# First layer's modulation in channel chunks, four column groups of TensorE, three projection units side by side

## The reference, cut to what matters

```python
cond_act = jax.nn.silu(cond)
shift, scale, gate = jnp.split(cond_act @ w_mod[layer] + b_mod[layer], 3, axis=-1)
hm = rmsnorm(x, norm_g[layer]) * (1 + scale[:, None]) + shift[:, None]
out = fc_mixer(hm, ...)      # layer 0: proj = h @ w_in, 1024 x 6144
x = x + gate[:, None] * out
```

## Time and profile before

| | |
|---|---|
| median of 3 runs | 1208.44 us (1207.91 to 1212.69) |
| profiled execution | 1208.46 us |
| its span | 1206.5 us |
| mean granted TensorE clock | 0.987 |
| TensorE busy | 94% |
| VectorE busy | 66% |
| ScalarE busy | 37% |
| GpSimd busy | 23% |
| HBM read | 134.31 MB |

### The profile page before, as it was taken

How to read it: one execution, slowest core, us unless ns; L and a number is a source line. 1 busy time by engine, 2 the same in 40 slices (tenths; PEclk the granted TensorE clock), 3 DMA queues, 4 the chain that set the end, 5 groups by cost and what they waited for, 6 DMA issues and landing times. The chain is left out here.

```text
span 1206.5 us, 19283 instructions
## 1 busy us (share of the span) xinstructions
PE 1134.3 (94%) x7179; PEld 1042.9 (86%) x7179; DVE 790.4 (66%) x1385; ACT 441.6 (37%) x846; POOL 279.9 (23%) x422
## 2 busy tenths in 40 slices
PE   6799999999999999999999999998999898978997
PEld 1389999999999998888899988998899898967885
DVE  1553444467666434547779796979797979776454
ACT  3331222121211123235534544453545354544321
POOL 1110000000000000013043533445353535454001
PEclk9899999999999999999999999999999999989999
DMA  8642223154544243314234333434342425272702
GB/s 332 190 145 69 85 87 104 54 180 123 169 127 152 88 162 105 95 35 157 72 101 131 101 112 106 127 102 126 93 122 85 131 76 156 68 268 65 298 26 87
DMA packets 175674, 148.11 MB, mean 123 GB/s; under 512 B 6844, under 2 KB 156708, under 8 KB 175220
## 3 DMA queue, kind: packets, MB, share of 16 engines
q1 hardware_dynamic: 170996, 130.29, 34.8%
q0 software_dynamic: 4608, 16.83, 4.2%
HBM read 134.31 MB, written 12.78 MB: 122 GB/s over the span
## 5 line engine op out<-in xcount | busy, mean ns | idle before, releaser
L261 DVE TENSOR_TENSOR w_lo<-raw_w,w_hi 128x1024 fp32r<-128x1024 f32 x128 | 157.0, 1230 | 94.4 <-ACT w_hi L255 92.8
L290 PE MATMUL PS<-h_hi,w_hi 128*128 128x320 f32 x768 | 177.0, 312 | 6.2 <-DVE h_lo L364 5.2
L290 PE MATMUL PS<-h_lo,w_hi 128*128 128x320 f32 x768 | 175.6, 310 | 0.0
L290 PE MATMUL PS<-h_hi,w_lo 128*128 128x320 f32 x768 | 175.4, 310 | 0.0
L255 ACT ACTIVATE w_hi<-raw_w 128x1024 fp32r<-128x1024 f32 x128 | 134.2, 1051 | 111.3 <-PE PS L290 72.2
L290 PEld LDWEIGHTS PS<-h_hi,w_hi 128*128 128x128 f32 x768 | 128.3, 188 | 11.3 <-issue 4.0
L1320 PE MATMUL PS<-h_hi,w_hi 128*128 128x320 f32 x480 | 118.9, 329 | 12.5 <-DVE big L1509 7.1
L290 PEld LDWEIGHTS PS<-h_hi,w_lo 128*128 128x128 f32 x768 | 129.0, 188 | 0.0
L290 PEld LDWEIGHTS PS<-h_lo,w_hi 128*128 128x128 f32 x768 | 128.9, 188 | 0.0
L1320 PE MATMUL PS<-h_hi,w_lo 128*128 128x320 f32 x480 | 111.4, 314 | 0.0
L1320 PE MATMUL PS<-h_lo,w_hi 128*128 128x320 f32 x480 | 111.1, 313 | 0.0
(11 more groups left out here) (223 smaller groups left out, 2250.2 us busy)
## 6 DMA issues: line engine op xcount, KB each, us to landing
raw_w<-in_fc_w_in_dram SPq DMA_DIRECT2D x48, 512.0 KB, 4.0
raw_w<-in_ssd_w_in_dram SPq DMA_DIRECT2D x48, 512.0 KB, 5.2
big<-l_scr SPq DMA_DIRECT2D x40, 512.0 KB, 4.3
big<-in_w_mod_dram POOLq DMA_DIRECT2D x16, 1024.0 KB, 5.4
raw_w<-in_fc_w_out_dram SPq DMA_DIRECT2D x16, 512.0 KB, 3.4
raw_w<-in_ssd_w_out_dram SPq DMA_DIRECT2D x16, 512.0 KB, 7.9
big<-in_w_mod_dram SPq DMA_DIRECT2D x6, 1024.0 KB, 18.0
y_scr<-big SPq DMA_DIRECT2D x40, 128.0 KB, 1.8
```

The source lines that it names most:

```text
L261: dve.tensor_tensor(w_lo[:, slot, :], raw_w[:, slot, :], w_hi[:, slot, :].bitcast(F32), ALU.subtract).then_inc(lo_ready, 1)
L290: mm = pe.matmul(PS[:, 2 * pair + s, 0:HALF], w[:, slot, ws], h[:, kt, s * HALF:(s + 1) * HALF], start=(kt == 0 and n == 0), stop=(kt == K ...
```

## The change

The eight pieces by k become four chunks by channels: chunk c holds shift and scale of channels 256c to 256c+255, for all eight k tiles (2 MB in two loads, rows of 1 KB). Two chunks fit in memory at once, so that chunks 2 and 3 wait until 0 and 1 are used.

- `mod_pe(c)`: eight matmuls, k tile t to column group t mod 4 (partitions 32q and up of PSUM bank 6), two k tiles added up in each group. The weights are the conditioning vectors padded with zeros to 32 columns (`condp`).
- `mod_copy_act(c)` copies the bank (128 by 512) to memory, and `mod_T_pe(c)` multiplies each 128 by 128 block of it by a new constant (`group_sum`), which adds the four groups and puts channels on partitions. `ss_dve(c)` makes scale and shift of two k tiles.
- Units 0, 1 and 2 run side by side in three pairs of PSUM banks, two k tiles at a time (`unit_part_pe`); chunk c+1's matmuls stand ahead of unit 0's part c, its sum between unit 0's and unit 1's. Unit 3 follows as before.
- The norm is done ahead of the modulation: SP loads x first, in five pieces, and ScalarE's queue the constants and conditioning vectors. Unit loads stand between chunks.
- On ScalarE `h_act` of the two k tiles of a chunk stands around the copy of the next chunk.

Other renamings and the waits that go with them are left out.

```diff
         xn = carve(5120 + 8192, 2, D)
         xT0 = carve(15360, KT, TOK)
-        mod_sb = carve(21504, 2 * D)
+        mod_sb = carve(25220, 2, 512)
         praw = carve(21504 + 2048, 2, P)
         praw3 = carve(23808, P)
...
-        def h_dve(dve, layer, xTb):
-            dve.wait_ge(xt_done, NT * (layer + 1) - 1)
-            dve.wait_ge(mod_ready, 2 * (layer + 1))
-            for k in range(KT):
-                for c, (a, b) in enumerate(SEGS):
-                    if k == 0 and c == 1:
-                        dve.wait_ge(xt_done, NT * (layer + 1))
-                    dve.tensor_scalar(xTb[:, k, a:b], xTb[:, k, a:b], ss_mod[:, 1, c, k:k + 1], ss_mod[:, 0, c, k:k + 1],
+        def ss_dve(dve, c):
+            ks = slice(2 * c, 2 * c + 2)
+            sel = PS[:, 7, 8 * c:8 * c + 8].rearrange("p (s k c) -> p s c k", s=2, c=2)
+            dve.wait_ge(mod_T, c + 1)
+            bias = par2[:, 56:72].rearrange("p (s k) -> p s k", s=2)[:, :, ks]
+            for s in range(2):
+                e = dve.tensor_tensor(ss_mod[:, s, :, ks], sel[:, s], bias[:, s].unsqueeze(1).to_broadcast([P, 2, 2]), ALU.add)
+            e.then_inc(ss_step, 1)
+            dve.wait_ge(ss_step, c + 1)
+            dve.scalar_tensor_tensor(out=ss_mod[:, 1, :, ks], in0=ss_mod[:, 1, :, ks], scalar=1.0,
+                                     in1=par2[:, ks].unsqueeze(1).to_broadcast([P, 2, 2]), op0=ALU.add, op1=ALU.mult).then_inc(ss_ready, 1)
+        def h_dve(dve, c):
+            dve.wait_ge(ss_ready, c + 1)
...
+                for seg, (a, b) in enumerate(SEGS):
+                    dve.tensor_scalar(xT0[:, k, a:b], xT0[:, k, a:b], ss_mod[:, 1, seg, k:k + 1], ss_mod[:, 0, seg, k:k + 1],
                                       ALU.mult, ALU.add).then_inc(v_done, 1)
-                if k % 2:
-                    dve.wait_ge(hh_done, KT * layer + k)
-                    dve.tensor_tensor(h_lo[:, k - 1, :], xTb[:, k - 1, :], h_hi[:, k - 1, :].bitcast(F32),
-                                      ALU.subtract).then_inc(h_ready, 1)
...
+            dve.wait_ge(hh_done, 2 * c + 1)
+            dve.tensor_tensor(h_lo[:, 2 * c, :], xT0[:, 2 * c, :], h_hi[:, 2 * c, :].bitcast(F32), ALU.subtract).then_inc(h_ready, 1)
...
+        def mod_pe(pe, c):
+            pe.wait_ge(wm_landed[c % 2], 32 * (c // 2) + 32)
+            if c:
+                pe.wait_ge(mod_copied, c)
+            for half in range(2):
+                for q in range(4):
+                    t = 4 * half + q
+                    mm = pe.matmul(PS[32 * q:32 * q + 32, 6, :].rearrange("p (s n) -> p s n", s=2), condp[:, t, :], wm[c % 2][:, :, t, :],
+                                   start=(half == 0), stop=(half == 1))
+            mm.then_inc(wm_used, 1)
+        def mod_T_pe(pe, c):
+            pe.wait_ge(mod_copied, c + 1)
+            if c:
+                pe.wait_ge(ss_step, c)
+            for j in range(4):
+                mm = pe.matmul(PS[:, 7, 8 * c + 2 * j:8 * c + 2 * j + 2], mod_sb[:, c % 2, j * P:(j + 1) * P], group_sum,
+                               start=True, stop=True)
+            mm.then_inc(mod_T, 1)
+        def mod_copy_act(act, c):
+            act.wait_ge(wm_used, c + 1)
+            if c >= 2:
+                act.wait_ge(mod_T, c - 1)
+            act.activation(mod_sb[:, c % 2, :], PS[:, 6, :], ACT.Copy).then_inc(mod_copied, 1)
+        def unit_part_pe(pe, u, c):
+            if c == 0:
+                pe.wait_ge(lo_ready, u + 1)
+            for kt in (2 * c, 2 * c + 1):
+                if u == 0:
+                    h_wait(pe, 0, kt)
+                ws = slice(kt * P, (kt + 1) * P)
+                for n, (w, h) in enumerate(((w_hi, h_hi), (w_hi, h_lo), (w_lo, h_hi))):
+                    for s in range(2):
+                        mm = pe.matmul(PS[:, 2 * u + s, 0:HALF], w[:, u, ws], h[:, kt, s * HALF:(s + 1) * HALF],
+                                       start=(kt == 0 and n == 0), stop=(kt == KT - 1 and n == 2))
...
         def start_pe(pe):
+            pe.wait_ge(cst_landed, 16)
+            for t in range(3):
+                norm_pe_tile(pe, t)
             pe.wait_ge(par_landed, 16 * PAR_DMAS)
             pe.transpose(PS[:, 6, 0:P], praw[:, 0, :], ident)
             pe.transpose(PS[:, 6, P:P + 72], praw[0:72, 1, :], ident[0:72, 0:72]).then_inc(par_T, 1)
-            pe.wait_ge(cond_ready, 1)
-            for s in range(8):
-                q, half = s // 2, s % 2
-                pe.wait_ge(wm_landed[s], 16)
-                for t in range(2):
-                    for b in range(2):
-                        mm = pe.matmul(PS[0:2, 2 * half + b, :], cond[:, :, 2 * q + t], wm[s][:, t, 512 * b:512 * b + 512],
-                                       start=(q == 0 and t == 0), stop=(q == 3 and t == 1))
-                mm.then_inc(wm_used, 1)
-                if 1 <= s < NT + 1:
-                    norm_pe_tile(pe, 0, xn, s - 1)
-        def start_pe_mod_T(pe):
-            pe.wait_ge(mod_copied, 2)
-            pe.wait_ge(xt_done, NT)
-            for j in range(16):
-                mm = pe.transpose(PS[:, 4, 2 * j:2 * j + 2], mod_sb[0:2, j * P:(j + 1) * P], ident[0:2, 0:2])
-            mm.then_inc(mod_T, 1)
+            for t in range(3, NT):
+                norm_pe_tile(pe, t)
+            pe.wait_ge(cond_padded, 1)
+            pe.wait_ge(par_ready, 2)
+            mod_pe(pe, 0)
+            mod_T_pe(pe, 0)
+            for c in range(4):
+                if c < 3:
+                    mod_pe(pe, c + 1)
+                unit_part_pe(pe, 0, c)
+                if c < 3:
+                    mod_T_pe(pe, c + 1)
+                unit_part_pe(pe, 1, c)
+                unit_part_pe(pe, 2, c)
         def fourier_pe(pe, i, first):
-            for k in range(4):
+            for k in range(3 if first else 0, 4):
                 pe.wait_ge(lo_ready, 4 * i + k + 1)
-                if not (first and k < 2):
-                    pe.wait_ge(act_freed, 4 * i + k - 1)
-                channel_tile(pe, k, k % 2, first and k == 0)
+                pe.wait_ge(act_freed, 4 * i + k - 1)
+                channel_tile(pe, k, k % 2)
...
-                src = pair_view(k % 2)
+                src = pair_view(2 if first and k == 2 else k % 2)
...
-            sp.dma_start(cond[:, 0, :], A["c"].rearrange("a (p t) -> (a p) t", t=KT)).then_inc(cond_landed, 16)
-            sp.dma_start(cond[:, 1, :], A["c_ctx"].rearrange("(p t) -> p t", t=KT)).then_inc(cond_landed, 16)
-            sp.dma_start(cst[:, :], A["consts"]).then_inc(par_landed, 16)
+            xs = A["x_sample"][0].rearrange("(t p) d -> p t d", p=P)
+            for t in range(NT):
+                sp.dma_start(x[:, t, :], xs[:, t, :] if t < 4 else A["x_prompt"][0]).then_inc(x_landed[t], 16)
             sp.dma_start(praw[0:96, 0, :], A["ssd_conv_w"].rearrange("a k (t n) -> (a k t) n", n=P)).then_inc(par_landed, 16)
             sp.dma_start(praw[96:128, 0, :], A["ssd_conv_b"].rearrange("a (t n) -> (a t) n", n=P)).then_inc(par_landed, 16)
             sp.dma_start(praw[0:16, 1, :], A["norm_g"].rearrange("a (t n) -> (a t) n", n=P)).then_inc(par_landed, 16)
             sp.dma_start(praw[16:40, 1, :], A["fc_conv_w"].rearrange("a k (t n) -> (a k t) n", n=P)).then_inc(par_landed, 16)
             sp.dma_start(praw[40:56, 1, :], A["ssd_norm_g"].rearrange("a (t n) -> (a t) n", n=P)).then_inc(par_landed, 16)
             sp.dma_start(praw[56:72, 1, :], A["b_mod"].rearrange("a (t n) -> (a t) n", n=P)[0:16, :]).then_inc(par_landed, 16)
-            xs = A["x_sample"][0].rearrange("(t p) d -> p t d", p=P)
-            for s in range(8):
-                if s == 7:
-                    sp.wait_ge(wm_used, 1)
-                q, half = s // 2, s % 2
-                sp.dma_start(wm[s], wm_src[0][:, 2 * q:2 * q + 2, 1024 * half:1024 * half + 1024]).then_inc(wm_landed[s], 16)
-                if s < 2:
-                    sp.dma_start(x[:, 2 * s:2 * s + 2, :], xs[:, 2 * s:2 * s + 2, :]).then_inc(x_landed[s], 16)
-                if s == 2:
-                    sp.dma_start(x[:, 4, :], A["x_prompt"][0]).then_inc(x_landed[2], 16)
-            for u in range(4):
-                if u % 2 == 0:
-                    sp.wait_ge(wm_used, 2 + u // 2)
+            def chunk_load(c):
+                if c >= 2:
+                    sp.wait_ge(wm_used, c - 1)
+                for s in range(2):
+                    sp.dma_start(wm[c % 2][:, s], wm_src[0][:, :, 1024 * s + 256 * c:1024 * s + 256 * c + 256]).then_inc(wm_landed[c % 2], 16)
+            def first_load(u):
                 sp.dma_start(raw_w[:, u, :], fc_src[:, :, fc_col(u):fc_col(u) + P]).then_inc(landed[u], 16)
-            sp.wait_ge(mod_ready, 2)
+            chunk_load(0)
+            first_load(0)
+            first_load(1)
+            chunk_load(1)
+            first_load(2)
+            chunk_load(2)
+            chunk_load(3)
+            first_load(3)
+            sp.wait_ge(wm_used, 4)
```

(82 more changed lines are left out.)

68 lines of the change are left out of this document (29 added, 39 removed).

## The result

| | before | after |
|---|---|---|
| median of 20 runs each, taken in turn | 1210.79 us | 1215.24 us |
| ratio, 95% interval | | 1.0035 (1.0022 to 1.0048) |
| the profiled execution, and its span | 1208.46, 1206.5 us | 1214.56, 1212.5 us |
| forecast | | 1194.5 us (1189.5 to 1202) |

The account below looks back on a forecast made before the run. TensorE, 94% busy and dense from about 64 us, was taken as the bound, with a serial start ahead. From 1208.46 us, 14.8 for an earlier third evacuation came off and 0.9 of gate stall was added: 1194.5 us (1189.5 to 1202).

Parts of the forecast that it names:

- a chunk's matmuls: Modulation on TensorE: two overlapping rounds of four matmuls, 1.95 us at full clock, 3.5 us at half clock.
- rival 3: Modulation matmuls: column groups do not overlap, 6.9 us a chunk, kernel slower at 1214 to 1221; chance 0.05.
- rival 2: Loads set the pace: 1 KB rows no faster than 512 B, chunk 1 at 28.2, total 1199; chance 0.15.
- The stall of PE: TensorE idle ahead of unit 0's odd k, waiting for copy, h_hi and h_lo: 2.2 us in each steady period.
- The gate weights: First gate weights, loaded by GpSimd after h, arrive late for VectorE and stall TensorE by 0.9 us.
- Chunk 0: First modulation chunk: landed at 16.3, matmuls from 17 to 20.5 at half clock, beside the loading of chunk 1.
- the whole sum: Start of the kernel: chunk 1, two periods and last round put the third evacuation at 63.85, 14.8 us earlier.
- Later iterations: Gate loads after the first have 0.7 us of margin and are untouched.
- rival 4: An unseen wait in the new order, likely on ScalarE, takes 8 us or more, around 1205; chance 0.07.
- rival 1: TensorE's clock falls in the new stalls, losing 1.75 us in each of four rounds, +7, 1201.5; chance 0.15.

Follow-up runs that it names:

- b_fill9: Kernel before with nine empty one-column memsets more at VectorE's start (loop at 507): 1217.41 us against 1211.18, ratio 1.0071.
- a_cut9: Kernel after with nine VectorE instructions fewer ahead of the loop (at 498, as before): 1206.01 us, 0.9954 to the kernel before.
- a_order_cut9: Kernel after with nine VectorE instructions fewer and ScalarE's odd-k rounding ahead of the next chunk's copy: 1195.33 us, 0.9868 to the kernel before.
- a_order_fill83: Kernel after with ScalarE's odd-k rounding ahead of the next chunk's copy and 83 empty VectorE memsets: 1191.46 us, 0.9846 to the kernel before.
- a_order: Kernel after with ScalarE's rounding of the odd k ahead of the copy of the next chunk: 1201.74 us, 0.9927 to the kernel before.
- a_warm: Kernel after with 14 unused matmuls ahead of each odd-k wait of unit 0 in three rounds: 1203.41 us, 0.9949 to the kernel before.

## Why the prediction was wrong, point by point

**What was right.** The mechanism of the change and most of its prices: a chunk's matmuls 1.92 and, cold, 3.64 us (1.95 and 3.5 forecast), so rival 3, column groups that don't overlap, falls; the copy 0.60 (0.6), h_hi 0.73 (0.73), h_lo 1.53 (1.55), sum and transposes 1.05 at full clock (0.9); 1 KB rows at 345 to 350 GB/s (351), chunk 1's matmuls at 26.70 (25.8), so rival 2, slow loads, falls too. The stall of PE was 1.88 us in later rounds (2.2). The gate weights cost 0.53 us ahead of L796 (0.9), and where the start is as fast as forecast or faster 1.4 to 2.2. Chunk 0 was wrong and hidden: its matmuls began at 20.68, not 17, and chunk 1's load covered that.

**What made the sign wrong.** The step that failed is the premise of the whole sum: "From about 64 us on PE is dense, so whatever is gained ahead of that shifts the rest one for one", and with it "Later iterations ... are untouched". Up to 695 the gain was passed on nearly in full (5.6 us at 84, 4.9 at 695). It was then lost to a cost that isn't in the operations at all: the nine instructions that the change adds to VectorE ahead of the loop moved its end over a border. I counted what each added instruction costs where it stands, some tenths of a microsecond beside other work, and never where all the instructions behind it come to lie. Two jumps at 5.2 us are 10.4 us of VectorE. The pairs of runs that differ in nothing but the place, or in little else, show 0.6 to 0.8% of the time (b_fill9 0.71; a_cut9 0.81; a_order_cut9 0.59 and a_order_fill83 0.81 against a_order), 7 to 10 us, so most of it reaches the end. None of my rivals was this: rival 4 left room for an unseen wait, but put it on ScalarE and priced it at 1205. At an equal place the time would have been about 1206 (a_cut9), outside my range as well.

**What made the size wrong.** The term that was mis-sized is the clock. The length of the stall was right; rival 1, that the clock falls in it, had 0.15 and 1.75 us a round, "Against: two thirds of each period are dense". It fell in every round that had a stall, three of them. The two later ones lost 3.1 and 2.8 us, the first 1.4, because the clock stayed at 0.50 for nearly 7 us of dense work (45.2 to 52.0, 58.9 to 65.7), where I had taken 3.5 us from the earlier trace rows. The same rows show it low from 47.8 to 54.6, 6.8 us in all. I had counted only the part behind the return of dense work, and in the new rounds PE is at work again when the clock falls. My case against it rested on one idle time of 1.03 us that had left the clock at 1.00. The stalls here were longer, 1.31 and 1.88 us; in the two later rounds the clock fell ahead of the two-column matmuls, and a_warm has the same two-column matmuls and no fall, so they alone don't bring it down. With a_warm's rounds the third evacuation stands at 65.79, against the 63.85 of the sum: of the other 1.9 us, 0.9 is chunk 1's later start; the rest I haven't traced. The clock thus explains 6.9 of the 8.8 us missed at that point.

**What I could have had.** The stall itself was in my text ("The odd k of unit 0 comes after modulation c+1 by: copy ..."), as a fact of the change. Moving one line takes it away, and with it the fall of the clock: 13.3 us, more than twice what the change gained. The clock and the stall weren't two risks but one chain.

## What to carry to other kernels

Ahead of a long hardware loop, count the instructions of each engine, of both kernels: an idle time put down to "issue" at a loop's jump, on an engine whose instruction queue has more packets than before, says, by these runs, that the loop now reaches into one block more, and the cure is some instructions fewer or, as cheaply, some empty ones more. Price a short stall of TensorE not by its length but by what the clock does behind it (here 1.9 us cost another 3), and look first whether another order of the engine that releases it takes it away. A comparison of two kernels should be made at an equal place, or it measures the place too: here it was worth more than the change.

## What the runs showed of the hardware that I had not expected

- A jump back in VectorE's loop of 329 instructions cost nothing, 3.3 to 3.5 or 5.0 to 5.3 us, depending on where the loop began; nine empty instructions 740 us earlier cost 6 us by the medians and 9 by the ratio (b_fill9), and 83 of them together saved some 0.8% (a_order_fill83 against a_order).
- TensorE's loop had an idle time of about 3 us at each jump in eleven kernels, the kernel before among them, and none in the one with 42 more matmuls ahead of it (a_warm).
- The clock fell to 0.50 behind idle times of 1.31 and 1.88 us. It stayed there for 3.4 us behind the first (35.0 to 38.4) and for 6.8 us behind each of the others, with PE busy without a gap.
- The conditioning's two loads of 4 KB took 5.6 and 7.0 us from issue to landing on ScalarE's queue, behind the constants (193 KB, 4.5 us) and beside x on SP's; before they took 1.6 to 1.7, ahead of everything. Which of the two held them up isn't shown. By the issues of the first 40 us of after (queue, count, size, us to landing):

```profile
cond<-in_c_dram ACTq DMA_DIRECT2D x1, 4.0 KB, 5.6
...
cond<-in_c_ctx_dram ACTq DMA_DIRECT2D x1, 4.0 KB, 7.0
```
